# The third attention of a four-layer program: probabilities stay unscaled, row sums come from products with ones, outputs are divided

## What is computed

```python
s = jnp.einsum('qgrd,qkgd->qgrk', q_blk, k_sel) * scale
s = jnp.where(valid[:, None, None, :], s, -jnp.inf)
p = jax.nn.softmax(s, axis=-1).astype(v_s.dtype)
return jnp.einsum('qgrk,qkgd->qgrd', p, v_sel)
```

## Time and profile before

| | us |
|---|---|
| median of 3 runs | 1283.51 |
| lowest and highest run | 1282.69, 1284.3 |
| profiled execution, first to last instruction | 1282.5 |
| TensorE busy with matmuls in it | 1261.1 (98%) |
| VectorE busy | 809.9 (63%) |
| ScalarE busy | 738.5 (58%) |
| GpSimd busy | 376.8 (29%) |

### The profile page before, as it was taken

One profiled execution on the slowest core, in us unless ns is written; L12 is line 12 of the kernel. 1 busy time (PEld: TensorE's weight loads), 2 busy tenths in 40 slices (PEclk: granted clock), 3 DMA queues, 4 the chain that ended last, 5 costly groups with the idle time before them and its releaser, 6 DMA issues.

```text
span 1282.5 us, 28401 instructions
## 1 busy us (share of the span) xinstructions
PE 1261.1 (98%) x10337; PEld 1215.3 (95%) x10337; DVE 809.9 (63%) x1422; ACT 738.5 (58%) x1375; POOL 376.8 (29%) x416
## 2 busy tenths in 40 slices
PE   6999999999999999999999899999999999999999
PEld 6988999999988999999989599999999889999999
DVE  5687755556576655557699875554547665755544
ACT  6576766654456566665566854443436776544433
POOL 2011344411000244431243127770100220677100
PEclk9999999999999999999999999999999999999999
DMA  7542555566654465566455045556555443655664
GB/s 265 177 136 87 190 186 184 183 208 200 215 174 151 153 193 181 192 194 205 154 185 171 9 150 181 178 170 191 168 177 181 151 139 100 192 186 182 196 191 154
DMA packets 66503, 220.55 MB, mean 172 GB/s; under 512 B 9312, under 2 KB 13808, under 8 KB 66288
## 3 DMA queue, kind: packets, MB, share of 16 engines
q1 hardware_dynamic: 64080, 212.77, 52.1%
q10 hardware_dynamic: 2336, 6.58, 1.7%
HBM read 215.61 MB, written 1.08 MB: 169 GB/s over the span
## 4 chain that ended last, share of the span: by engine, by line
PE 77%; issue 10%; POOL 5%; DVE 4%; ACT 3%; DMA 0%; POOLq 0%; ACTq 0%; SPq 0%; DVEq 0%
PE bank L341 23%; PE bank L343 22%; PE bank L342 22%; POOL scratch L581 1%; POOL scratch L583 1%; DVE wlo L325 1%; PE bank L930 1%; PE bank L915 1%; POOL alo L585 1%; ACT whi L320 1%; DVE scratch L571 1%; ACT ahi L556 1%; PE bank L912 1%; ACT prob L968 1%; PE bank L355 1%
## 5 line engine op out<-in xcount | busy, mean ns | idle before, releaser
L325 DVE TENSOR_TENSOR wlo<-raw,whi 128x1024 fp32r<-128x1024 f32 (+1 forms) x394 | 484.0, 1229 | 162.0 <-ACT whi L320 161.2
L341 PE MATMUL bank<-uhi,whi 128*128 128x256 f32 (+1 forms) x1848 | 532.8, 288 | 11.4 <-DVE wlo L325 10.7
L343 PE MATMUL bank<-uhi,wlo 128*128 128x256 f32 (+1 forms) x1848 | 525.0, 284 | 0.0
L342 PE MATMUL bank<-ulo,whi 128*128 128x256 f32 (+1 forms) x1848 | 524.3, 284 | 0.0
L320 ACT ACTIVATE whi<-raw 128x1024 fp32r<-128x1024 f32 (+1 forms) x394 | 410.6, 1045 | 183.7 <-PE bank L343 175.4
L341 PEld LDWEIGHTS bank<-uhi,whi 128*128 128x128 f32 x1848 | 349.8, 189 | 19.4 <-issue 17.1
L343 PEld LDWEIGHTS bank<-uhi,wlo 128*128 128x128 f32 x1848 | 350.1, 189 | 0.0
L342 PEld LDWEIGHTS bank<-ulo,whi 128*128 128x128 f32 x1848 | 348.7, 189 | 0.6
L341 PE MATMUL bank<-ahi,whi 128*128 128x256 f32 (+1 forms) x1168 | 332.9, 285 | 0.4 <-DVE wlo L325 0.4
L343 PE MATMUL bank<-ahi,wlo 128*128 128x256 f32 (+1 forms) x1168 | 330.6, 283 | 0.0
L342 PE MATMUL bank<-alo,whi 128*128 128x256 f32 (+1 forms) x1168 | 330.3, 283 | 0.0
(11 more groups left out here) (286 smaller groups left out, 1245.8 us busy)
## 6 DMA issues: line engine op xcount, KB each, us to landing
raw<-stream SPq DMA_DIRECT2D x394, 512.0 KB, 3.6
scratch<-decay ACTq DMA_DIRECT2D x8, 416.0 KB, 3.7
scratch<-relh ACTq DMA_DIRECT2D x8, 384.0 KB, 3.4
scratch<-scratch SPq DMA_DIRECT2D x68, 34.0 KB, 2.5
constants<-consts SPq DMA_DIRECT2D x1, 1296.0 KB, 11.1
h<-xT SPq DMA_DIRECT2D x4, 256.0 KB, 5.7
out<-h SPq DMA_DIRECT2D x8, 128.0 KB, 3.5
scratch<-scratch SPq DMA_DIRECT2D x16, 16.0 KB, 2.9
```

What stands on the lines that cost most here:

```text
L325: dve.tensor_tensor(wlo[:, s, 0:w], raw[:, s, 0:w], whi[:, s, 0:w].bitcast(F32), ALU.subtract).then_inc(w_lo, 1)
L341: pe.matmul(dst, hi, a, start=first and i == 0, stop=False)
L342: pe.matmul(dst, hi, b, start=False, stop=False)
L343: mm = pe.matmul(dst, lo, a, start=False, stop=last and i == chunks - 1)
```

## The change

The probabilities of the third layer's pairs stay as the exponentials leave them. The exponentials have no `accum_out` any more, the transposes wait on them alone (`p_exp`), and `pair_scale_dve` is gone from this layer. After the products with the values, TensorE multiplies a block of ones (128 x 64) with the same transposed probabilities into columns 256 to 511 of bank 0: so each of the 64 partitions of a head holds the row sums. VectorE then takes the reciprocal of these 128 x 256 numbers (`out_recip`), multiplies the output with it into a new buffer in SBUF (`out_f`, two slots), and ScalarE and VectorE take high and low part from there (`scaled_hi`, `scaled_lo`). The values of the next pair wait for the multiplication (`o_scaled`) and no longer for the low part. The other layers stay as they were.

```diff
--- before.py
+++ after.py
@@ -228,6 +228,8 @@
         hq = area(K0 + 4 * T + 896, 160).rearrange("p (c n) -> p c n", n=20)
         cosg = area(E0 + 1760 + 2 * T, T)
         nhq = area(E0 + 1760 + 3 * T, 32)
+        out_recip = area(E0 + 1760 + T, 256)
+        out_f = area(V0 + 9 * T, 512).rearrange("p (b n) -> p b n", b=2)
 
         gate, egate, tgate, mval = (
             area(K0 + 2 * T * i, 2 * T).rearrange("p (b t) -> p b t", b=2) for i in range(4))
@@ -286,8 +288,8 @@
         y_sq, y_stat, y_rstd, y_norm, y_cos, y_sin, y_turned, y_done = sems(
             "y_sq y_stat y_rstd y_norm y_cos y_sin y_turned y_done")
         y_swapped = sems("y_swapped0 y_swapped1 y_swapped2 y_swapped3")
-        s_ready, s_max, p_exp, p_norm, pt_ready, pt_copied, o_ready, o_hi, o_lo = sems(
-            "s_ready s_max p_exp p_norm pt_ready pt_copied o_ready o_hi o_lo")
+        s_ready, s_max, p_exp, p_norm, pt_ready, pt_copied, o_ready, o_recip, o_scaled, o_hi, o_lo = sems(
+            "s_ready s_max p_exp p_norm pt_ready pt_copied o_ready o_recip o_scaled o_hi o_lo")
         z_ready, z_log, z_split, z_masked, z_sum, z_arg, z_exp, z_w, z_o, z_ohi, z_olo = sems(
             "z_ready z_log z_split z_masked z_sum z_arg z_exp z_w z_o z_ohi z_olo")
         c_ready, c_stored, c_masked, meta_copied = sems("c_ready c_stored c_masked meta_copied")
@@ -823,7 +825,10 @@
 
         def turn_pe(pe, a, i):
             hd, p, dst = a.head0 + i, a.bufs[i % a.n], bank[6 + i % 2]
-            pe.wait_ge(p_norm, 2 * (hd + 1))
+            if a is dsa:
+                pe.wait_ge(p_exp, 2 * (hd + 1))
+            else:
+                pe.wait_ge(p_norm, 2 * (hd + 1 - (2 * dsa.pairs if a is fox else 0)))
             if hd - 1 > 0:
                 pe.wait_ge(pt_copied, hd - 1)
             idn = const("ident")
@@ -843,6 +848,20 @@
             act.wait_ge(o_ready, pr + 1)
             act.activation(ahi[:, a.chunk0 + s, a.cols], a.obank[:, 0:256], ACT.Copy).then_inc(o_hi, 1)
 
+        def scaled_hi(act, s):
+            act.wait_ge(o_scaled, s + 1)
+            act.activation(ahi[:, s, 0:256], out_f[:, s % 2, :], ACT.Copy).then_inc(o_hi, 1)
+
+        def out_scale_dve(dve, s):
+            dve.wait_ge(o_ready, dsa.head0 // 2 + s + 1)
+            dve.reciprocal(out_recip, dsa.obank[:, 256:512]).then_inc(o_recip, 1)
+            dve.wait_ge(o_recip, s + 1)
+            dve.tensor_tensor(out_f[:, s % 2, :], dsa.obank[:, 0:256], out_recip, ALU.mult).then_inc(o_scaled, 1)
+
+        def scaled_lo(dve, s):
+            dve.wait_ge(o_hi, dsa.head0 // 2 + s + 1)
+            dve.tensor_tensor(alo[:, s, 0:256], out_f[:, s % 2, :], ahi[:, s, 0:256].bitcast(F32), ALU.subtract).then_inc(o_lo, 1)
+
         def turned_act(act, a, i):
             hd = a.head0 + i
             act.wait_ge(pt_ready, hd + 1)
@@ -917,7 +936,9 @@
 
         def pair_values_pe(pe, a, s):
             pr, pair = a.head0 // 2 + s, (2 * s, 2 * s + 1)
-            if pr > 0:
+            if a is dsa and s > 0:
+                pe.wait_ge(o_scaled, s)
+            elif pr > 0:
                 pe.wait_ge(o_lo, pr)
             pe.wait_ge(pt_copied, a.head0 + 2 * s + 2)
             dst = [a.obank[64 * i:64 * i + 64, :] for i in range(2)]
@@ -931,6 +952,12 @@
             for i in pair:
                 mm = pe.matmul(dst[i % 2][:, 128:256], a.v(i, 1), a.pt[:, i % 2, 256:384], start=False, stop=True,
                                skip_group_check=True)
+            if a is dsa:
+                for i in pair:
+                    pe.matmul(dst[i % 2][:, 256:512], ones[:, 0:64], a.pt[:, i % 2, 0:256], start=True, stop=False, skip_group_check=True)
+                for i in pair:
+                    mm = pe.matmul(dst[i % 2][:, 384:512], ones[:, 0:64], a.pt[:, i % 2, 256:384], start=False, stop=True,
+                                   skip_group_check=True)
             mm.then_inc(o_ready, 1)
 
         def pair_turn_pe(pe, a, s):
@@ -965,8 +992,11 @@
                 act.wait_ge(s_max, 2 * (a.head0 + i + 1))
                 for t, (c0, w) in enumerate(((0, a.w0), (a.w0, a.w1))):
                     p = a.bufs[i % a.n][:, c0:c0 + w]
-                    act.activation(p, p, ACT.Exp, scale=-1.0, bias=a.nmx[:, i % a.n, t:t + 1],
-                                   accum_out=a.ssum[:, i % a.n, t:t + 1]).then_inc(p_exp, 1)
+                    if a is dsa:
+                        act.activation(p, p, ACT.Exp, scale=-1.0, bias=a.nmx[:, i % a.n, t:t + 1]).then_inc(p_exp, 1)
+                    else:
+                        act.activation(p, p, ACT.Exp, scale=-1.0, bias=a.nmx[:, i % a.n, t:t + 1],
+                                       accum_out=a.ssum[:, i % a.n, t:t + 1]).then_inc(p_exp, 1)
 
         def pair_turned_act(act, a, s):
             for i in (2 * s, 2 * s + 1):
@@ -1998,15 +2028,15 @@
             pair_biased_exp_act(act, a, 0)
             rms(18)
             rms(19)
-            for s in range(1, 10):
+            for s in range(1, 11):
+                if s >= 3:
+                    scaled_hi(act, s - 3)
                 if s < 8:
                     pair_biased_exp_act(act, a, s)
                 if s == 5:
                     tail_exp_act(act, 1)
                 if s in (4, 8):
                     tail_out_act(act, s // 5)
-                if s >= 2:
-                    out_hi(act, a, s - 2)
                 if s <= 8:
                     pair_turned_act(act, a, s - 1)
                 if s == 1:
@@ -2131,9 +2161,9 @@
                 if s == 5:
                     tail_max_dve(dve, 1)
                 if 3 <= s <= 8:
-                    out_lo(dve, a, s - 3)
-                if 1 <= s <= 8:
-                    pair_scale_dve(dve, link, a, s - 1)
+                    scaled_lo(dve, s - 3)
+                if 2 <= s <= 8:
+                    out_scale_dve(dve, s - 2)
                 if s == 1:
                     second(18)
                     second(19)
@@ -2145,8 +2175,11 @@
                 if s == 8:
                     split_lo(dve, At(START["out2"] + 1))
                     split_lo(dve, At(START["out2"] + 2))
-                if s >= 8:
-                    out_lo(dve, a, s - 2)
+                if s == 8:
+                    scaled_lo(dve, 6)
+                if s == 9:
+                    out_scale_dve(dve, 7)
+                    scaled_lo(dve, 7)
                 if s == 2:
                     tail_queries(1)
                 if s == 8:
```

## The result

The changed kernel takes 1297.62 us (median; 1297.42 to 1301.24), the one before 1283.55 us beside it: a ratio of 1.0115 with a 95% interval of 1.0102 to 1.0128. It is 14.1 us slower. Forecast were 1294.0 us with a range of 1286.5 to 1299.5, and slower with a chance of 0.88.

The account below looks back on a forecast made before the run. The prediction took TensorE's stream, busy from unit to unit, as the bound. To 1283.5 us it added 10.2 for the pairs' longer loop and 0.3 for a half-clock window: 1294.0 us, range 1286.5 to 1299.5.

Parts of the forecast that it names:

- The reciprocal's price: VectorE's 128x256 reciprocal: 0.157 us plus 255 further columns at 0.006 each, 1.69 us; ends kept at 0.42 and 2.45.
- The sums: TensorE's products with ones: four more matmuls, 0.80 us for each pair and 6.4 us in all.
- Rival C: Sums fit into TensorE's waits and the reciprocal streams, so the kernel gets faster: about 1280 us; chance 0.04.
- The start: Before the first values: ScalarE's removed reads of sums let them start 0.74 us earlier, at 714.28.
- The loop: Pairs: values wait for the previous pair's product and reciprocal; eight stretches make matmuls with pair 7 start 10.2 us later.
- Stretches 1 and 5: Reciprocal, tail scaling and transposes, then values and sums, with scores only in the first: 5.80 and 4.94 us.
- rival A: The reciprocal streams in 0.42 us, so pair 7 starts 3.6 us later: 1287.1 us; chance 0.22.
- the signs: Expected in the profile: TensorE waits at L951, tail pieces and before pair 7's matmuls; pair 7's values at 753 to 754.
- The clock: TensorE idling more brings half-clock windows, one costing 1.4 us on certain stretches; 0.3 us added for the chance.
- stretches 2, 6 or 7: Two TensorE-paced stretches of 4.43 and 4.49 us and the projection's of 9.86, where a half-clock window costs 1.4.
- B: The reciprocal costs 9 ns a column, 2.45 us, making VectorE's step the loop: +15.2 us, 1298.7; chance 0.22.
- D: Reads of the sums stay in ScalarE's stream, costing the 0.74 us of the start: 1294.7 us; chance 0.02.

Follow-up runs that it names:

- e8_warm8: Changed kernel with 8 idle products, results unread, on TensorE in front of the tail's transposes in steps 2 and 6; 1296.73 us.
- e1_plain: Changed kernel with the 128x256 reciprocal replaced by a multiplication with 1.0 of the same shape; 1288.01 us.
- after: The changed kernel itself, as profiled after the change, against the kernel before; 1297.62 us, ratio 1.0115.
- e2_nosums: Changed kernel without the four products with ones of each pair, reciprocal kept but reading the outputs; 1292.95 us.
- e4_pool: Kernel before the change, with the scaling of pairs 1 to 7 moved from VectorE to GpSimd; 1288.85 us.

## Why the prediction was right, and where its sizes were off

It was right in direction and mechanism, and 3.6 us short, with the measured time inside the range.

- **The reciprocal's price.** Taken 1.69 us, measured 1.76: 6.3 ns a column instead of 6. That it came so close is in part luck: the 6 ns are the difference of a mean of 163 ns, which mixes the medians 157 and 166 of two stages, to the 157 ns of one column, and single ones scatter from 152 to 169 ns. It was the step trusted least. That it is an iterated operation, and so dearer than a product, fits: 1758 against 425 ns at the same shape. 0.07 us more in six stretches is 0.4 of what was missing.
- **The sums.** 0.80 a pair, measured from start to start 0.75 (726.39 to 727.14), and little hid them: left out, they give back 4.7 to 6.0 of 6.0 us. Rival C is out.
- **The start.** The removed reads of sums were to bring the first values 0.74 us earlier. Counted from the scores that begin at 706.75 and, before, at 706.84, they start after 7.44 us (714.19) instead of 8.18 (715.02): 0.74.
- **The loop.** The eight stretches, from reciprocal to reciprocal, as laid out and as measured:

| | 1 | 2 | 3 | 4 | 5 | 6 | 7 | 8 |
|---|---|---|---|---|---|---|---|---|
| laid out | 5.80 | 4.43 | 5.74 | 3.93 | 4.94 | 4.49 | 9.86 | 3.15 |
| measured | 7.22 | 4.28 | 5.69 | 3.84 | 6.31 | 4.22 | 10.01 | 3.27 |
| with 8 fillers (`e8_warm8`) | 5.59 | 4.29 | 5.68 | 3.84 | 4.73 | 4.23 | 10.01 | 3.28 |
| streaming instead (`e1_plain`) | 4.26 | 4.29 | 4.34 | 3.11 | 3.40 | 4.24 | 8.83 | 1.94 |

  Six are within 0.3 us. Stretches 1 and 5 are 1.4 us longer each, and both hold a half-clock window; with the 8 fillers, without one there, all eight are within 0.3. The last row is rival A's layout to within 0.3 us as well. Of the signs, the waits at the tail's pieces and in front of pair 7 came as drawn; at L951 there was one of 0.7 us only. The values of pair 7 started at 755.75, later than the 753 to 754 named, by the two windows.
- **The clock: the term that was mis-sized.** "I add 0.3 for the chance of one" put the window on stretches 2, 6 or 7, with no price for one elsewhere. Two came, just behind the two waits of 2 us, in stretches 1 and 5. In stretch 1 TensorE has scores, values and sums to do behind the tail's transposes, in stretch 5 values and sums, and VectorE's next reciprocal waits for exactly these. A slowed TensorE is on the path there. 2.8 us instead of 0.3 is most of the difference (3.2 by the run with 8 fillers). The prediction also tied such windows to TensorE's waits; the windows at 710 to 715 us in ten profiles, which come without a wait ahead of them, show that this is not the whole rule.
- **The rest.** 10.2 laid out, 2.8 for the clock, 0.4 for the reciprocal and -1.0 for all else give the 12.4 us at the matmuls with pair 7. Then come 0.9 more inside the span, where the gap at L343 is, and 0.8 by which the profiled execution of the kernel before was over its median: 14.1 in all. The prediction had neither of these two. That a delay of TensorE's stream here is a delay of the end, held: nothing of it was made good later.
- **The rivals.** A lies 9.6 us away and was made by an experiment; its layout, 1287.1, was 0.9 too low. B's 1298.7 is nearer to the measured time than my forecast, but that is chance: its 9 ns a column are refuted, and it was the clock that filled the gap. D is refuted: ScalarE has 32 instructions less on the page (1343, before 1375), which are the reads of two sums for each of 16 heads, and the first reciprocal starts at 715.75 where 715.97 was laid out.

## What to carry over

Dividing the output instead of the probabilities saves columns only if the divisor is small. Here it made 16 reciprocals of two columns (0.16 us each) into 8 of 256 (1.76 us each), since every sum stood in all 64 rows of its head. Price a reciprocal by its columns, and not as a product of that shape. And before an operation is put between the end of one product and the start of the next, list what stands behind it in its engine's queue: the largest waits of the changed kernel were charged to lines that the change had not touched, and in the form with ScalarE the order of its queue alone was worth 6.1 us. Last, a profile is one execution: look at the granted clock of the other runs before a difference of 1 or 2 us is put down to an edit.

## What the runs showed of the hardware

- A reciprocal on VectorE is linear in the columns at 6.25 ns each: 152 to 157 ns for one column, 958 for 128, 1758 for 256. A product of 128x256 out of PSUM takes 425 ns.
- On ScalarE a logarithm and an exponential of 128x256 take 0.38 and 0.42 us, together less than half of VectorE's reciprocal of the same shape.
- GpSimd's product with a column of factors takes 606 ns for 128 columns and 928 for 256. VectorE's two products of a head together take 0.55 us.
- Every profile has a window of clock 0.50 between 709 and 723 us, with or without a change: in ten of the twelve it starts at 709.5 to 712.5, with no wait of TensorE listed from 660 us on, and in the other two behind a wait of 1.5 and 2.0 us. Where TensorE is the path one costs 1.3 to 1.6 us.
- The same wait is followed by such a window in one kernel and not in another: behind the wait of 1.97 us at the tail's transposes `after` has one, and behind one of 1.98 us at the same place `e2_nosums` has none. In the profiled executions on this stage a mean clock of 0.999 goes with one window, 0.997 with two and 0.996 with three (`e4_pool`, with one of its three 7 us long, has 0.994). So a change that makes TensorE wait can cost more than the wait, and a single profile doesn't tell whether it will.
